# A streaming encoder layer: a 128-byte filler tile goes, and the input norm gets two small tiles of its own

## What is computed

```
xn = rmsnorm(x)                       # x * rsqrt(mean(x*x) + eps) * gain
qkv, z, a, b, sq, sk, sv, ... = split(xn @ w_in)      # 1024 x 3336
mix = [gated DeltaNet | sliding-window attention | gated short convolution]
h = x + mix @ w_o
h = h + memory_attention(rmsnorm(h), mem_k, mem_v)    # projections w_mq, w_mo
u = causal_conv3(rmsnorm(h) @ w_up)                   # 1024 x 5632
h = h + (silu(u_gate) * u_value) @ w_down             # 2816 x 1024
```

## Time and profile before

| what | us |
|---|---|
| median of 3 runs | 1935.7 |
| lowest and highest of the 3 | 1929.4, 1936.65 |
| the profiled execution's own time | 1935.7 |
| its span, from first to last instruction | 1934.4 |

### The profile page before, as it was taken

How to read it: one execution, slowest core, us unless ns; L and a number is a source line. 1 busy time by engine, 2 the same in 40 slices (tenths; PEclk the granted TensorE clock), 3 DMA queues, 4 the chain that set the end, 5 groups by cost and what they waited for, 6 DMA issues and landing times. The chain is left out here.

```text
span 1934.4 us, 27945 instructions
## 1 busy us (share of the span) xinstructions
PE 1839.3 (95%) x10427; PEld 1684.8 (87%) x10427; DVE 1165.7 (60%) x1367; ACT 787.6 (41%) x1499; POOL 736.6 (38%) x650
## 2 busy tenths in 40 slices
PE   5999999999988999999998997999999999999999
PEld 4989889998966788898888877999999999988787
DVE  4224555665656642423415238888887888699985
ACT  4114664315675442311124226444444444544432
POOL 3001222005434260121113405666666666547643
PEclk9999999999999999999999999999999999999999
DMA  5121212214143340112431122222222222496554
GB/s 158 43 56 35 59 34 57 70 59 138 56 120 112 118 187 22 44 66 84 178 120 48 62 66 73 69 78 69 68 68 78 70 77 68 156 329 212 161 170 149
DMA packets 159034, 188.07 MB, mean 97 GB/s; under 512 B 13809, under 2 KB 112730, under 8 KB 158520
## 3 DMA queue, kind: packets, MB, share of 16 engines
q1 hardware_dynamic: 157156, 186.30, 29.6%
q10 hardware_dynamic: 884, 0.25, 0.1%
q0 software_dynamic: 896, 0.19, 0.1%
HBM read 151.64 MB, written 35.07 MB: 97 GB/s over the span
## 5 line engine op out<-in xcount | busy, mean ns | idle before, releaser
L3573 PE MATMUL ffn_banks<-h_parts,up_hi 128*128 128x384 f32 x1920 | 491.7, 337 | 10.3 <-POOL h_parts L3977 4.3
L3573 PEld LDWEIGHTS ffn_banks<-h_parts,up_hi 128*128 128x128 f32 x1920 | 348.3, 189 | 11.7 <-issue 7.2
L3573 PE MATMUL ffn_banks<-h_parts,up_lo 128*128 128x384 f32 x960 | 322.3, 336 | 0.0
L3973 POOL TENSOR_TENSOR up_lo<-up_raw,up_hi 128x512 fp32r<-128x512 f32 x174 | 254.6, 1478 | 136.4 <-ACT up_hi L3735 136.3
L921 PE MATMUL proj_banks<-x_hi,in_w_hi 128*128 128x384 f32 (+1 forms) x648 | 223.7, 345 | 4.3 <-DVE room L1308 4.3
L921 PE MATMUL proj_banks<-x_lo,in_w_hi 128*128 128x384 f32 (+1 forms) x648 | 218.2, 337 | 0.0
L921 PE MATMUL proj_banks<-x_hi,in_w_lo 128*128 128x384 f32 (+1 forms) x648 | 218.2, 337 | 0.0
L3573 PEld LDWEIGHTS ffn_banks<-h_parts,up_lo 128*128 128x128 f32 x960 | 181.6, 189 | 0.0
L4024 POOL TENSOR_TENSOR h_parts<-down_cells,h_parts 128x512 fp32r<-128x512 f32 x69 | 111.0, 1616 | 90.3 <-ACT h_parts L3808 90.3
L3694 PE MATMUL ffn_banks<-h_parts,up_hi 128*128 128x512 f32 x352 | 138.3, 393 | 3.8 <-DVE h L4241 2.3
L3697 PE MATMUL ffn_banks<-h_parts,up_lo 128*128 128x512 f32 x352 | 137.1, 390 | 0.0
(11 more groups left out here) (515 smaller groups left out, 3904.4 us busy)
## 6 DMA issues: line engine op xcount, KB each, us to landing
up_raw<-in_w_up SPq DMA_DIRECT2D x44, 512.0 KB, 3.9
down_cells<-in_w_down SPq DMA_DIRECT2D x58, 256.0 KB, 5.2
up_raw<-ffn_gated_rows SPq DMA_DIRECT2D x44, 320.0 KB, 5.4
ffn_gated_rows<-h SPq DMA_DIRECT2D x22, 576.0 KB, 2.8
in_w_raw<-in_w_in SPq DMA_DIRECT2D x24, 512.0 KB, 3.8
up_raw<-ffn_gated_rows SPq DMA_DIRECT2D x44, 256.0 KB, 3.3
mem_k_one<-in_cache_mem_k SPq DMA_DIRECT2D x8, 1024.0 KB, 4.9
spill<-mixT SPq DMA_DIRECT2D x10, 576.0 KB, 3.9
```

The lines of the kernel that those rows point to most:

```text
L3573: ins = nc.tensor.matmul(banks[:, bank, 0:TC], wt[:, j, k, :], parts[:, q, x, k, :], start=(fresh and n == 1), stop=(n == last), skip_grou ...
L3973: nc.gpsimd.tensor_tensor(w_lo[:, j], weights.full(j), w_hi[:, j].bitcast(F32), ALU.subtract).then_inc(weights.split[j], 1)
```

## The change

`NormParts` no longer takes the shared `C.root` and `C.inv` for its root and inverse, but makes two [128, 9] tiles in the phase of its stage. Its only user is `InputNorm` in `in_projection`. The tile `level` is no longer made.

```diff
@@ NormParts.__init__
         self.xn = xn.rearrange("p (i t d) -> p i t d", i=2, t=self.GROUP)
-        self.root, self.inv = C.root, C.inv
+        self.root, self.inv = (ph.sb(f"{tag}_{n}", [P, NT]) for n in ("root", "inv"))
         self.rooted, self.inverted, self.scaled, self.turned, self.high, self.low = (
@@ program
         C.a_log, C.dt_bias, C.sinks, C.eps = (C.sb(n, [P, 4]) for n in ("a_log", "dt_bias", "sinks", "eps"))
 
-        C.sb("level", [P, 32])
         C.state_stored, C.window_stored, C.memory_stored, C.y_stored = (
```

## The result

The changed kernel took 1945.71 us, the median of six executions (1942.41 to 1949.15), against 1935.87 us (1929.4 to 1941.16) for the kernel before. The ratio is 1.0053, with a 95% interval of 1.0032 to 1.0075: slower by 10.3 us (6 to 14.5). The forecast was 1935.7, with a range up to 1944. The profiled execution was itself on the low side, 1941.18 us, with a span of 1939.8 against 1934.4.

A forecast was written before the change was run, and what follows sets the result against it. The prediction took TensorE's rate to bound nearly all of the kernel, busy 1839.3 of 1934.4 us. Terms of 0 for new tiles, TensorE, other engines and transfers left 1935.7 + 0 = 1935.7 us, range 1927 to 1944.

The forecast's parts named there:

- the one headed TensorE: All matmuls: shifting the left stack 128 bytes costs 0, bound 1 ns in 379, 4.9 us in either direction.
- The new tiles: Input norm's roots, reciprocals and scalings write or read other bytes: 0, at most 0.1 us either way.
- VectorE, ScalarE and GpSimd: Their instructions on shifted left-stack tiles: 0; in the last stage 0.5, 0.7 and 0.3 us possible.
- Transfers: Loads at the start, prompt rows to `kv`: 0, at most 3.0 us either way; stores from `h` an estimated 2.6% less.
- The waits: TensorE's waits before the change: 16.4 us at the start for small vectors, then 3.2 (L226), 2.3 and 1.6 (L4241).
- The sum: Whole kernel: 0 for new tiles, TensorE, three other engines and transfers, 1935.7 + 0 = 1935.7 us.
- The slower one: Last stage: more VectorE and GpSimd collisions between tiles 128 apart, 12 us on the path, 1947.7 us; chance 0.09.
- The faster one: Last stage and start: TensorE's idle 7.15 us and 3.0 us of transfers won, 1925.5 us; chance 0.06.
- the layout that does not act: Left stack: filler's room taken up by rounding or tiles standing where nothing is, so 1935.7 us; chance 0.01.
- the lower level: Whole kernel: falls to the level of one earlier run for no reason in the change, 1929.4 us; chance 0.10.
- A median of a matmul that has moved by 2 ns or more: Sign in the changed profile that the forecast is wrong: 2 ns on each of 10427 matmuls are 20.9 us.

The follow-up runs named there:

- e4: Program of float32r matmuls alone, weight or moving tile shifted in 32-byte steps: 173.3 to 176.7 ns with w_b to w_i; 110.8 to 111.7 ns at 128 columns.
- e2: Kernel before, filler kept, input norm's root and inverse written into it, so new tiles without a shift: 1934.06 us, ratio 0.9993.
- e5: Kernel before with 128 bytes of filler behind up_lo, moving only ffn_part_sums and ffn_room: 1934.53 us, ratio 1.0006.
- e1: Kernel before with the filler tile made in the right stack instead of the left, both stacks starting at 96 by 256: 1934.35 us, ratio 0.9992.
- e6: Changed kernel with filler ahead of up_hi, putting up_hi and up_lo back at 224, other left tiles staying at 96: 1936.24 us, ratio 1.0011.
- e3: Kernel before with 128 bytes of filler ahead of up_hi in the feed-forward stage alone: 1944.03 us, ratio 1.0042.
- e7: Program of matmuls alone, all 64 pairs of eight weight and eight moving starts: 173.3 and 226.7 ns at distance 0, 176.0 and 232.2 to 233.3 at 128.

## Why the prediction was wrong

**The step that failed** is the one headed TensorE: "So the shift costs 0; the bound is 1 ns in 379, 0.26%, which over 1839.3 us is 4.9 us". The shift costs 2.3 to 2.6 ns in 173 and 5.4 in 227, up to 2.4%, in 5880 of the 10427 matmuls: 17.7 us of TensorE's time. The prediction saw the one fact that counts, that `up_hi` and `h_parts` would stand 128 bytes apart, and then priced it by four rows that could not show it, for three reasons:

- The rows were of other forms. The matmuls of the earlier trace rows have 128 or 256 columns, the three stages 384 or 512. By e4 the interval at 128 columns is the same at all starts. L2989 and L2962 multiply plain float32 at an interval of 216 ns, where 256 columns of float32r took 113 to 120 in the probe; their 379 ns stand for another pace.
- Duration was read in place of the interval. Successive matmuls overlap, and two medians of 379 ns say little on how soon the next one starts. The number that mattered was in the earlier trace rows already, 475 us for 2730 matmuls.
- No pair was 128 apart. L3035 has its inputs 96 apart, and all of the large products had theirs at distance 0. A row that holds the variable still bounds nothing. With nothing to go by, the honest bound was an open one, and the upper end of 1944 too low. That it was missed by only 1.7 us is no merit of the working: it was made of this bound, which bounds nothing, and of 3.0 us for transfers that cost none.

**The new tiles** at 0: right, by e2 (0.9993) and by the rows of nx_root and nx_inv, 166 and 298 ns.

**VectorE, ScalarE and GpSimd** at 0: right as far as it was tried. L1145 still lies between 1435 and 1447 ns at its new starts, and e5 moved two tiles of theirs in the feed-forward part for 1.0006.

**Transfers** at 0: right within what can be told. `kv` and `h` are at 96 in e1 and e6; e1 has 0.9992, and e6 has no more than the input projection's matmuls explain. The first wait of TensorE is 15.9 us for 16.4. By the rule of the Trainium skill that the prediction cited ("DMA: Bandwidth & Descriptors", section "How a descriptor splits into AXI transactions"), stores from `h` would cost a little less. No run here shows that: the 22 stores `ffn_gated_rows<-h` take a median of 2.8 us to landing in both profiles. The prediction's reason, that such stores end nobody's wait, isn't quite so: the last wait of the DMA queue, 1.6 us, is for `out_y_sample<-h`, and an estimate of 2.6% of that is 0.04 us.

**The waits** of TensorE were read with one left out: the earlier trace rows has 4.3 us for GpSimd's `h_parts` (L3977), longer than the 3.2 that the prediction names second. It was 4.3 after the change too, so nothing hangs on it.

**The sum** of 0 was off by 10.3 us. Of the 17.7 us of added matmul time, a part was paid for out of waits for VectorE and others, which shrank while TensorE was at work longer. The down-projection shows it best. In the profiled executions its matmul intervals, waits included, add up to 244.9 us for 242.7, 2.1 more, for 5.7 us of longer matmuls: there TensorE also waits for VectorE, and the intervals over 300 ns, which hold those waits, went from 9.5 us in all to 5.7. In the up-projection it is 5.8 us more for 7.5. A part of what is hidden in the feed-forward stages may be the clock's instead: the profiled execution of the changed kernel has one stretch of 3.4 us at a granted clock of 0.5 (1.2 GHz) less there. By itself each part was timed in e3 (the two feed-forward stages, +8.1) and e6 (the input projection, +2.1); up- and down-projection were not timed apart.

**The rivals.** The slower one had the sign and not the mechanism: VectorE's rows in the last stage did not move, and more than half of the loss sits in the up-projection, most of which is the loop, where the prediction saw the most cover and TensorE had none to give. The faster one, the layout that does not act and the lower level fall by the result, the fastest of the six being 1942.41 us. "A median of a matmul that has moved by 2 ns or more" was named as a sign, at 20.9 us for all; the page's means moved by 3 to 5 ns in just the three stages.

## What to carry to other kernels

Where TensorE runs without a gap, anything that can touch the pace of a matmul goes ahead of all covers, and a layout that moves one operand against the other is such a thing: for each product look at the distance of the two starts by 256 bytes, and keep it at 0 if the layout allows it. Price such an edit by the interval between starts, the count of matmuls in a stretch without waits, on rows of the same width and type, and ask of every row whether the variable was different in it at all. In this kernel a filler tile that nothing reads was worth 10 us.

## What the runs showed of the hardware

- Float32r matmuls of 384 columns take 173.3 to 176.7 ns and those of 512 take 226.7 to 234.5 ns, depending on the distance between the starts of weights and moving tile, with a period of 256 bytes (e4, e7). Plain float32 was not tried. For 512 columns only the distance 0 is best, and the moving tile 64 above the weights is next (228.9).
- The Trainium skill ("SBUF — State Buffer", section "Who interferes with whom") gives TensorE two read ports, one for the moving operand and one for the weight load, and calls them independent. The probe does not bear that out in full: with no other engine at work, where the two tiles stand against each other makes up to 3.4 ns of 173.3. What in the memory or the engine does this stays open, and whether it is the two reads that meet; the runs vary the addresses and cannot see the cause.
- At one distance (the moving tile 32 above the weights) the same program runs the loop at 173.3 ns in one execution and 176.7 in another. The probes have both rates at 96 below the weights too, and at 64 below once 173.3 in place of 174.7. What decides was not tried.
- Distance 0 doesn't always give the best pace. The product for the memory's keys and values (L2195, 512 columns, both operands in the left stack at 128, then at 0) has a mean interval of 231.4 ns before and after, in single values from 224 to 240, and not 226.7. What holds it up was not looked into; that it did not change is as the distance has it.
- No layout tried beats the kernel before: it has distance 0, than which the map has nothing better, in all three large stages.
